# Twelve more of layer 0's weight blocks in split form, with later splits behind fp32 blocks and POOL's clears cut into pieces

## The chip, the cores and the metric

The kernel runs on one core of one Trainium2 chip. The metric is the device time of one launch in microseconds. The core has TensorE (PE, matrix products), VectorE (DVE), ScalarE (ACT), GpSimd (POOL) and SyncE (SP, which here only issues DMAs). Each engine works through its own instruction queue in order; they meet through semaphores.

## The reference

One inference step of a two-layer decoder trunk on 264 token columns (256 of a prompt, 8 samples). Per layer:

```
proj = x @ w_in                                   # 1024 -> 2816, cut into HGRN2 | retention | S5 inputs
o_hg, s_hg = chunked gated linear recurrence      # 6 heads, state 64 x 64
o_rt, s_rt = retention (rotary q, k)              # 6 heads
y5, s5     = complex diagonal S5 scan, gelu, glu
mixed = concat(o_hg, o_rt, y5) @ w_out
x = layer_norm(ALPHA * x + mixed)
ff = square(relu(x @ w_up)) @ w_down
x = layer_norm(ALPHA * x + ff)
```

The outputs are x of both layers' end and the new states. All is fp32, with D_MODEL 1024 and D_FF 4096.

## The kernel before

**Weight blocks.** All dense weights come as 192 blocks of 128 x 1024 fp32 (512 KB), 96 for each layer: steps 0 to 23 are `w_in` (N_IN = 24), then 8 of `w_out`, and the MLP. SP loads block n into `w_raw` slot n % 3 (L480). One step of the schedule is one block; between blocks PE works small "units" of the mixers (levels of the recurrence, scores, transposes, state products), placed by hand in PLAN.

**Two forms.** An fp32 block multiplies `w_raw` with X directly, in 8 matmuls that the profile shows as 16 passes (L971). A split block is written as w = w_high + w_low in fp32r: ACT copies the high part (`split_high`, L1048), DVE subtracts the low part (`split_low`, L1494), and PE does 24 fp32r matmuls (L995 to L997: high by high, high by low of the activations, low by high). Activations are split likewise into `a_high` and `a_low` (L1499). UNSPLIT lists the fp32 blocks of each layer: before, blocks 0 to 21 and 23 of layer 0; layer 1 has none, so all its blocks are split.

**When a block's buffer comes free.** SP loads block n when block n - 3 has been read: a split one as soon as `split_low` is through (`low_ready`), an fp32 one only when PE has finished it (`chunk_done`), see `wait_raw_read`. ACT and DVE issue the split of block n at the head of step n - 2 (AHEAD = 2), in front of that step's own work. That own work, `mixer_work(l, c)` on either engine, evacuates tile c - 1 (gates, Q products, K, V), copies unit results out of the four mix banks and frees these banks for PE (`unit_free`), and frees the three stream banks (`tile_free`).

**DVE's queue in layer 0.** Ahead of step 0: softmax terms, the first table pieces, the eight `a_low` subtractions, more softmax terms. Steps 0 to 9: the S5 tables in pieces (PIECES), and from step 6 on the Q products (L1651), which free the stream banks of tiles 5, 6 and 7. Steps 13 and 14: the two S5 halves (`s5_half`). Steps 10 to 17: the recurrence's levels (L1731 to L1747), rotary, S5 states, gelu argument; steps 16 to 18: `hgrn_sample_add` (L1776), each of which frees a mix bank that `ret_score` (L837) takes later.

**ACT in steps 20 to 22.** Step 20 copies the outputs of `hg_o`, which frees the bank of `hg_state` (L767); step 22 has `head_root` (a square root, with a table load) and eight small copies of the retention's sample outputs (L1245, L1246), for which `ret_mu` (L878) waits. `split_high(22)` and `split_high(24)` stand ahead of these.

**POOL's queue.** Constants and states are loaded by DMAs from POOL; it also clears `s5_near`, `near_packed`, `near` (1536 columns, L520), `st_p` (320, L521) and `level_space` (3072, L522) at the start, each counted in `cleared`. Later it makes the own-value blocks (`affine_select`, L506).

Of the kernel before, what the change touches and what calls it, by code (L numbers as in the profile page):

```python
# [14 lines left out]
DEPTH = 2  # L15
# [5 lines left out]
KT = D_MODEL // 128  # L21
# [24 lines left out]
N_CHUNKS = DOWN_B + 2 * KT  # L46
FF_HALF = FF_TILES // 2
CHUNK = 8 * 128
RAW_SLOTS = 3
SPLIT_SLOTS = 3  # L50
AHEAD = 2
# [113 lines left out]
    if _at[1][0] not in BY_ROW_TILE:  # L165
        UNITS_DONE[_at] = len(UNITS_DONE) + 1
MIX_BANKS = 4
UNSPLIT = ((0, 1, 2, 3, 4, 5, 6, 7, 8, 9, 10, 11, 12, 13, 14, 15, 16, 17, 18, 19, 20, 21, 23), ())
SPLIT = [_n % N_CHUNKS not in UNSPLIT[_n // N_CHUNKS] for _n in range(DEPTH * N_CHUNKS)]
FIRST_SPLIT = [min(_c for _c in range(N_CHUNKS) if _c not in UNSPLIT[_l]) for _l in range(DEPTH)]  # L170
BY_POOL = 3
# [5 lines left out]
def build(nc, xT, weights, vectors, matrices, constants, level_masks, state_hg, state_rt, state_s5,  # L177
          y_out, hg_p_out, rt_p_out, s5_p_out, hg_s_out, rt_s_out, s5_s_out):
    with ExitStack() as ctx:
# [263 lines left out]
        def need(eng, s, n):  # L443

            if n > 0:
                eng.wait_ge(s, n)

        def split_count(n):

            return sum(SPLIT[:n + 1])  # L450
# [37 lines left out]
        def _(pool):  # L488
# [28 lines left out]
            pool.dma_start(consts[:, 0:a], constants[:, 0:a]).then_inc(const_loaded, 16)  # L517
            pool.dma_start(masks[:, :, :], level_masks).then_inc(const_loaded, 16)
            pool.dma_start(s5x0[:, :, :, :, :], state_s5).then_inc(const_loaded, 16)
            pool.memset(near[:, :, :, :, :], 0.0).then_inc(cleared, 1)  # L520
            pool.memset(st_p[:, :, :], 0.0).then_inc(cleared, 1)  # L521
            pool.memset(level_space, 0.0).then_inc(cleared, 1)  # L522
            for l in range(DEPTH):
                if l == 0:
                    pool.wait_ge(chunk_done, 1)
# [502 lines left out]
        def _(act):  # L1028
# [12 lines left out]
            def split_high(n):  # L1041

                if n >= DEPTH * N_CHUNKS or not SPLIT[n]:
                    return
                wait_raw(act, n)
                if n >= SPLIT_SLOTS:
                    act.wait_ge(chunk_done, n - SPLIT_SLOTS + 1)
                act.activation(w_high[:, n % SPLIT_SLOTS, :], w_raw[:, n % RAW_SLOTS, :], ACT.Copy).then_inc(high_ready, 1)  # L1048
# [356 lines left out]
            split_high(1)  # L1405
            for l in range(DEPTH):
                for c in range(N_CHUNKS):
                    split_high(l * N_CHUNKS + c + AHEAD)
                    if c < N_IN:
                        mixer_work(l, c)  # L1410
                        if l and c in (1, 2, 3, 4):
                            ln2_output(l - 1, 2 * c - 2)
                            ln2_output(l - 1, 2 * c - 1)
                        if l == 0 and c == ROT_AT:
                            s5_rot(0)
                        if c == N_IN - 1:
                            mixer_end(l)
                    elif c <= UP_A:
                        ln1_step(l, c)
                    elif c <= DOWN_A:  # L1420
                        m = c - 1 - UP_A
                        linear_sums(l, m)
                        if m == 0:
                            ln1_deviation(l)
                        else:
                            linear_hidden(l, m - 1)
                        if c == DOWN_A:
                            linear_hidden(l, m)
                        if c == UP_A + 3 and l + 1 < DEPTH:
                            act.wait_ge(table_ready, l + 1)  # L1430
                            s5_dt(l + 1)
                        if c == UP_A + 12 and l + 1 < DEPTH:
                            s5_sin(l + 1)
                    elif c < UP_B:
                        if c == DOWN_A + 1:
                            ln1_output(l, 0)
                        elif (c - DOWN_A) % 2 == 0:
                            ln1_output(l, (c - DOWN_A) // 2)
                        if c == DOWN_A + 11 and l + 1 < DEPTH:
                            s5_rot(l + 1)  # L1440
                    elif UP_B < c <= DOWN_B:
                        hidden(l, c - 1 - UP_B + FF_HALF)
                    if c > DOWN_B:
                        ln2_step(l, c)
                    if c in (TABLES_AT + 1, TABLES_AT + 2) and l + 1 < DEPTH:
                        table_copies(l, l + 1, c - TABLES_AT - 1)
                norm(l)
# [3 lines left out]
        def _(dve):  # L1451
# [44 lines left out]
            def split_a(l, part, k, src, m):  # L1496

                dve.wait_ge(ahigh_ready, 24 * l + 8 * part + k + 1)
                put(tt(a_low[:, m, :], src[:, m, :], a_high[:, m, :].bitcast(F32), ALU.subtract), a_ready)  # L1499
# [571 lines left out]

            pieces(2)
            split_low(0)
            for m in range(KT):
                split_a(0, 0, m, X, m)
            split_low(1)
            dve.wait_ge(softmax_exp, 1)
            chain(tt(low[:, 4, :], low[:, 0, :], low[:, 1, :], ALU.add))
# [9 lines left out]

            for l in range(DEPTH):
                for c in range(N_CHUNKS):  # L2090
                    split_low(l * N_CHUNKS + c + AHEAD)
                    if l == 0 and c < TABLE_STEPS:
                        pieces(PIECES[c])
                    if l == 0 and c == TABLE_STEPS:
                        run(first_table)
                        dve.wait_ge(const_loaded, 48)
                    if c < N_IN:
                        mixer_work(l, c)
                        if c == N_IN - 1:
                            mixer_end(l)  # L2100
                    elif c <= UP_A:
                        ln1_step(l, c)
                        if c == UP_A:
                            table = s5_tables(l + 1) if l + 1 < DEPTH else iter(())
                    elif c <= DOWN_A:
                        m = c - 1 - UP_A
                        linear(l, m)
                        if m:
                            hidden_low(l, m - 1)
                        if c == DOWN_A:  # L2110
                            hidden_low(l, m)
                            ln1_scale(l, 0)
                    elif c < UP_B:
                        m = (c - DOWN_A) // 2
                        if (c - DOWN_A) % 2:
                            if m + 1 < KT:
                                ln1_scale(l, m + 1)
                            split_a(l, 2, m, X1, m)
                        else:
                            half_down(l, m - 1)  # L2120
                    elif c <= DOWN_B:
                        if c == UP_B:
                            half_down(l, KT - 1)
                        else:
                            hidden(l, c - 1 - UP_B + FF_HALF)
                            hidden_low(l, c - 1 - UP_B + FF_HALF)
                    else:
                        ln2_step(l, c)
                    if c in TABLE_PIECES:
                        next(table, None)  # L2130
                    if c == TABLES_AT:
                        run(table)
                    if c == N_CHUNKS - 1:
                        residual_down(l, KT - 1)
                norm(l)
# [142 lines left out]
```

## Time and profile before

| | |
|---|---|
| median of 3 runs | 819.85 us (819.52 to 824.4) |
| profiled execution | 821.55 us |
| its span, first to last instruction | 819.5 us |
| mean granted TensorE clock | 0.958 |
| PE busy, share of the span | 754.9 us, 92% |
| DVE busy | 557.6 us, 68% |
| ACT busy | 394.8 us, 48% |
| POOL busy | 43.9 us, 5% |

A busy share is a mean over stages with different limits, so the timelines of the engines in one stretch say more than it does. A row of a timeline gives the start in us, the time taken, the engine, the line of the kernel, the operation, what it writes and reads, and how often it follows itself; in brackets stands how long the engine was idle before and what ended it. A clock of 1.00 is 2.4 GHz, 0.50 is 1.2 GHz.

### The profile page before, as it was taken

The page shows a single profiled execution, that of the slowest core. Times are in us where ns is not written, and L with a number is a line of the kernel's source. Part 1 is how long each engine was busy: PE and PEld are TensorE (multiplying, and loading weights), DVE is VectorE, ACT ScalarE, POOL GpSimd, SP SyncE. Part 2 cuts the span into 40 slices and gives each one's busy share as a digit, 9 for nine tenths or more (in the row PEclk, how much of TensorE's full clock was granted, in tenths as well). Part 3 has the DMA queues.
Part 4 walks back from the last instruction along what each step waited for, and adds up shares of the span by engine and source line. Part 5 has one row for each costly group of instructions (what it writes and reads, how often), then busy time and mean ns, then how long its engine had stood idle before and what let it go on. Part 6 is the DMA issues. An engine that isn't in the chain of part 4 may idle for free. (4 is left out here: it accounts for less than half of the span.)

```text
span 819.5 us, 18059 instructions
## 1 busy us (share of the span) xinstructions
PE 754.9 (92%) x7478; PEld 704.5 (86%) x7478; DVE 557.6 (68%) x1041; ACT 394.8 (48%) x743; POOL 43.9 (5%) x54
## 2 busy tenths in 40 slices
PE   6999798889999999989978899798999999999994
PEld 5788577779999999889978887687899999999994
DVE  7976962246688898884545999635477886666554
ACT  3522214245487654446437525254356874455342
POOL 4000102100000000000021002010000000000001
PEclk9999799888999999999998999899799999999998
DMA  8531112624355555444443232323244555555531
GB/s 343 190 109 54 54 54 93 226 78 141 117 172 164 168 169 178 156 155 154 155 129 104 80 117 94 120 78 112 72 135 154 182 171 190 181 178 169 194 104 53
DMA packets 31009, 113.58 MB, mean 139 GB/s; under 512 B 3568, under 2 KB 3776, under 8 KB 30544
## 3 DMA queue, kind: packets, MB, share of 16 engines
q1 hardware_dynamic: 28368, 101.83, 38.4%
q0 software_dynamic: 1984, 9.52, 3.0%
q8 instruction: 59, 0.97, 0.5%
q10 hardware_dynamic: 576, 1.08, 0.4%
q14 instruction: 22, 0.18, 0.1%
HBM read 108.24 MB, written 4.18 MB: 137 GB/s over the span
## 5 line engine op out<-in xcount | busy, mean ns | idle before, releaser
L1494 DVE TENSOR_TENSOR w_low<-w_raw,w_high 128x1024 fp32r<-128x1024 f32 x169 | 208.5, 1233 | 145.5 <-ACT w_high L1048 144.0
L1048 ACT ACTIVATE w_high<-w_raw 128x1024 fp32r<-128x1024 f32 x169 | 178.1, 1054 | 174.3 <-PE stream L997 146.9
L995 PE MATMUL stream<-a_high,w_high 128*128 128x264 f32 x584 | 176.9, 303 | 14.6 <-DVE a_low L2058 6.3
L996 PE MATMUL stream<-a_low,w_high 128*128 128x264 f32 x584 | 170.9, 293 | 0.0
L997 PE MATMUL stream<-a_high,w_low 128*128 128x264 f32 x584 | 170.3, 292 | 0.0
L995 PE MATMUL stream<-h_high,w_high 128*128 128x264 f32 x512 | 147.8, 289 | 1.3 <-issue 0.6
L996 PE MATMUL stream<-h_low,w_high 128*128 128x264 f32 x512 | 145.2, 284 | 0.0
L997 PE MATMUL stream<-h_high,w_low 128*128 128x264 f32 x512 | 145.0, 283 | 0.0
L995 PEld LDWEIGHTS stream<-a_high,w_high 128*128 128x128 f32 x584 | 115.3, 197 | 21.1 <-issue 16.8
L996 PEld LDWEIGHTS stream<-a_low,w_high 128*128 128x128 f32 x584 | 115.6, 198 | 0.3
L997 PEld LDWEIGHTS stream<-a_high,w_low 128*128 128x128 f32 x584 | 114.8, 197 | 0.0
L971 PE MATMUL stream<-X,w_raw 128*128 128x264 f32 x368 | 91.6, 407 | 8.6 <-DMA w_raw<-in_weights 7.6
L995 PEld LDWEIGHTS stream<-h_high,w_high 128*128 128x128 f32 x512 | 96.4, 188 | 3.2 <-issue 1.4
L996 PEld LDWEIGHTS stream<-h_low,w_high 128*128 128x128 f32 x512 | 96.5, 188 | 0.3
L997 PEld LDWEIGHTS stream<-h_high,w_low 128*128 128x128 f32 x512 | 96.0, 188 | 0.0
L971 PEld LDWEIGHTS stream<-X,w_raw 128*128 128x128 f32 x368 | 72.3, 200 | 23.6 <-DMA w_raw<-in_weights 8.1
L995 PE MATMUL stream<-pre_a,w_high 128*128 128x266 f32 x256 | 74.6, 291 | 1.7 <-DVEq L1473 1.7
L997 PE MATMUL stream<-pre_a,w_low 128*128 128x266 f32 x256 | 73.4, 287 | 0.0
L996 PE MATMUL stream<-pre_x,w_high 128*128 128x266 f32 x192 | 54.9, 286 | 0.0
L995 PEld LDWEIGHTS stream<-pre_a,w_high 128*128 128x128 f32 x256 | 48.4, 189 | 2.3 <-DVEq L1473 2.1
L997 PEld LDWEIGHTS stream<-pre_a,w_low 128*128 128x128 f32 x256 | 48.4, 189 | 0.0
L2029 DVE TENSOR_TENSOR h_low<-h_full,h_high 128x264 fp32r<-128x264 f32 x64 | 27.5, 430 | 18.1 <-ACT h_high L1390 15.7
(373 smaller groups left out, 1020.5 us busy)
## 6 DMA issues: line engine op xcount, KB each, us to landing
w_raw<-in_weights SPq DMA_DIRECT2D x192, 512.0 KB, 3.5
mats<-in_matrices POOLq DMA_DIRECT2D x2, 1024.0 KB, 5.7
S_hg<-in_state_hg POOLq DMA_DIRECT2D x2, 768.0 KB, 7.6
out_hg_s<-S_hg POOLq DMA_DIRECT2D x2, 768.0 KB, 3.7
consts<-in_constants POOLq DMA_DIRECT2D x1, 1484.5 KB, 9.4
X<-in_xT ACTq DMA_DIRECT2D x4, 264.0 KB, 5.1
out_y<-X SPq DMA_DIRECT2D x4, 264.0 KB, 2.1
S_rt<-in_state_rt POOLq DMA_DIRECT2D x2, 512.0 KB, 9.9
```

The costliest lines, as they stand in the source:

```text
L971: mm = pe.matmul(bnk[:, 0:T], w_raw[:, n % RAW_SLOTS, 128 * k:128 * k + 128], X[:, k, :], start=(k == 0), stop=(k == 7))
L995: pe.matmul(bnk[:, 0:width], wh, xh, start=(first and kk == 0), stop=False)
L996: pe.matmul(bnk[:, 0:width], wh, xl, start=False, stop=False)
L997: mm = pe.matmul(bnk[:, 0:width], wl, xh, start=False, stop=(last and kk == 7))
L1048: act.activation(w_high[:, n % SPLIT_SLOTS, :], w_raw[:, n % RAW_SLOTS, :], ACT.Copy).then_inc(high_ready, 1)
L1494: put(tt(w_low[:, n % SPLIT_SLOTS, :], w_raw[:, n % RAW_SLOTS, :], w_high[:, n % SPLIT_SLOTS, :].bitcast(F32), ALU.subtract), low_ready)
L2029: put(tt(h_low[:, m % FF_HALF, :], h_full[:, m % 2, :], h_high[:, m % FF_HALF, :].bitcast(F32), ALU.subtract), h_ready)
```

## The change

UNSPLIT for layer 0 becomes blocks 0 to 4, 6, 7, 9, 10, 12 and 13; blocks 5, 8, 11, 14 to 21 and 23 are split in addition to 22. FIRST_SPLIT of layer 0 goes from 22 to 5 with it. A split whose raw buffer is freed by an fp32 block (n - 3 unsplit: `split_late`) is issued at the head of step n - 1 in place of n - 2, on ACT and DVE alike; this holds for blocks 5, 15 and 16. The eight `a_low` subtractions move from the front of DVE's queue to step 2 of layer 0. POOL clears `near` in four pieces of 384 columns and `level_space` in twelve of 256; `cleared` counts as before.

```diff
-UNSPLIT = ((0, 1, 2, 3, 4, 5, 6, 7, 8, 9, 10, 11, 12, 13, 14, 15, 16, 17, 18, 19, 20, 21, 23), ())
+UNSPLIT = ((0, 1, 2, 3, 4, 6, 7, 9, 10, 12, 13), ())
@@
+        def split_late(n):
+
+            return RAW_SLOTS <= n < DEPTH * N_CHUNKS and not SPLIT[n - RAW_SLOTS]
+
@@ POOL
-            pool.memset(near[:, :, :, :, :], 0.0).then_inc(cleared, 1)
+            for h in range(2):
+                for t in range(2):
+                    m = pool.memset(near[:, h, :, t, :], 0.0)
+            m.then_inc(cleared, 1)
             pool.memset(st_p[:, :, :], 0.0).then_inc(cleared, 1)
-            pool.memset(level_space, 0.0).then_inc(cleared, 1)
+            for at in range(0, 3072, 256):
+                m = pool.memset(level_space[:, at:at + 256], 0.0)
+            m.then_inc(cleared, 1)
@@ ACT
-                    split_high(l * N_CHUNKS + c + AHEAD)
+                    n = l * N_CHUNKS + c
+                    if split_late(n + 1):
+                        split_high(n + 1)
+                    if not split_late(n + AHEAD):
+                        split_high(n + AHEAD)
@@ DVE
             pieces(2)
             split_low(0)
-            for m in range(KT):
-                split_a(0, 0, m, X, m)
             split_low(1)
@@
-                    split_low(l * N_CHUNKS + c + AHEAD)
+                    n = l * N_CHUNKS + c
+                    if split_late(n + 1):
+                        split_low(n + 1)
+                    if not split_late(n + AHEAD):
+                        split_low(n + AHEAD)
+                    if l == 0 and c == max(FIRST_SPLIT[0] - 3, 0):
+                        for m in range(KT):
+                            split_a(0, 0, m, X, m)
```

## Rows read from the trace of the kernel before

**Rows 1.** Busy time by stretch; columns: stretch, length, PE, PEld, DVE, ACT, POOL, clock, DMA
```profile
17.00:40.00 23.00, 22.00 (x98) 18.50 (x99) 21.13 (x63) 11.65 (x24) 0.00 (x0) 1.00 0.61 217
...
155.00:175.00 20.00, 15.28 (x86) 12.47 (x87) 8.19 (x16) 9.44 (x24) 0.00 (x0) 0.79 0.23 92
```

**Rows 2.** Timeline of PE and DVE, layer 0, blocks 2 to 8
```profile
16.95 21.63 PE L971 MATMUL stream<-X,w_raw 128*128 128x264 f32 x96 [1.59 <-DMA w_raw<-in_weights]
39.58 3.83 PE L971 MATMUL stream<-X,w_raw 128*128 128x264 f32 x16 [1.00 <-DVEq L1473]
...
32.67 0.69 DVE L1600 TENSOR_TENSOR scratch<-late,par 128x512 f32<-128x512 f32 x1
...
39.04 0.43 DVE L1651 TENSOR_TENSOR Qg<-Qg,stream 128x264 f32<-128x264 f32 x1
```

**Rows 3.** Waits up to 160 us (total, times, longest); PE's timeline, layer 0, late steps
```profile
ACT w_high L1048 <- DMA w_raw<-in_weights: 20.1, 2, 12.0
...
137.97 0.92 PE L767 MATMUL mix<-V_tok,scratch 128*64 128x64 f32 x24 [2.02 <-ACTq L1039]
...
163.74 3.01 PE L878 MATMUL mix<-MIX,consts 128*128 128x264 f32 x6 [3.35 <-ACT MIX L1246]
```

**Rows 4.** PE's timeline: fp32 block 13 of layer 0, split block 13 of layer 1
```profile
72.47 3.83 PE L971 MATMUL stream<-X,w_raw 128*128 128x264 f32 x16
76.13 1.89 PE L622 MATMUL mix<-scratch,late 128*128 128x64 f32 x16
...
500.03 0.39 PE L995 MATMUL stream<-a_high,w_high 128*128 128x264 f32 x1
...
503.13 0.46 PE L744 MATMUL mix<-scratch 64*32 64x32 f32 x32
```

**Rows 5.** The page's costliest groups: busy us, mean ns of one, idle before
```profile
L1494 DVE TENSOR_TENSOR w_low<-w_raw,w_high 128x1024 fp32r<-128x1024 f32 x169 | 208.5, 1233 | 145.5 <-ACT w_high L1048 144.0
L1048 ACT ACTIVATE w_high<-w_raw 128x1024 fp32r<-128x1024 f32 x169 | 178.1, 1054 | 174.3 <-PE stream L997 146.9
```

**Rows 6.** Timeline of DVE and POOL at the clears (`st_p`'s stands between the two)
```profile
8.94 4.76 DVE L1527 TENSOR_SCALAR par<-par 128x8 f32<-128x8 f32 x1
...
9.37 1.40 POOL L520 MEMSET near<- 128x1536 f32 x1
...
10.99 2.68 POOL L522 MEMSET scratch<- 128x3072 f32 x1
```

**Rows 7.** Timeline of DVE and POOL at the affine_selects
```profile
100.02 1.59 DVE L1756 TENSOR_TENSOR X<-X,consts 128x528 f32<-128x528 f32 x1
...
101.01 3.06 POOL L506 TENSOR_SCALAR_AFFINE_SELECT late<-late 8x1024 f32<-8x1024 f32 x2
```

**Rows 8.** Timeline of DVE and PE, layer 0, steps 12 to 17
```profile
64.74 0.64 DVE L1747 COPY_PREDICATED near_packed<-masks,mix 128x192 f32<-128x192 uint8 x2 [7.89 <-PE mix L744]
...
109.60 0.69 DVE L1776 TENSOR_TENSOR S_hg<-S_hg,mix 128x512 f32<-128x512 f32 x1 [0.93 <-PE mix L777]
...
110.49 0.70 PE L837 MATMUL mix<-QR,KR 32*128 32x256 f32 x4 [0.41 <-DVEq L1473]
```

**Rows 9.** PE's timelines, scores of step 18 in both layers, layer 1's steps 17 and 20
```profile
126.58 0.70 PE L837 MATMUL mix<-QR,KR 32*128 32x256 f32 x4 [0.63 <-ACTq L1039]
...
526.40 0.57 PE L995 MATMUL stream<-a_high,w_high 128*128 128x264 f32 x1
...
530.58 0.70 PE L837 MATMUL mix<-QR,KR 32*128 32x256 f32 x4
...
542.66 0.70 PE L837 MATMUL mix<-QR,KR 32*128 32x256 f32 x4 [1.28 <-ACTq L1039]
...
555.73 0.44 PE L862 MATMUL mix<-scratch,V_tok 128*64 128x128 f32 x4 [1.18 <-DVEq L1473]
```

**Rows 10.** PE's timeline, layer 0, behind block 17
```profile
115.10 1.07 PE L777 MATMUL mix<-late 8*64 8x512 f32 x4
...
117.11 0.70 PE L837 MATMUL mix<-QR,KR 32*128 32x256 f32 x4
```

## Prediction

> **What bounds the kernel.** I read the page's busy shares first: TensorE (PE) leads, VectorE (DVE) and ScalarE (ACT) are far behind. That is a mean over stages. The table by stretches shows what the mean hides: from 17 to 40 us DVE is busy for 21.13 of 23.00 us, nearly as full as PE, and from 155 to 175 us PE is busy for only 15.28 of 20.00 us at a mean clock of 0.79 [rows 1]. So I read the two ends of layer 0's mixer stage in the timelines, asking at each PE wait which engine ends it.
>
> Early, PE runs blocks 2 to 7 without a gap, 21.63 us from 16.95, or 3.6 us each, and block 8 then waits 1.00 us for DVE: its stream bank still holds tile 5, which DVE frees behind the product at 39.04 [rows 2]. Late, PE waits 2.02 us ahead of `hg_state` and 3.35 us ahead of `ret_mu`, both for copies that ACT makes behind a split whose raw block has not landed: those two split waits are 20.1 us of idle ACT, one of them 12.0 us [rows 3]. These two waits are what the change can remove outright.
>
> **What a split block costs and gives.** PE's own price, from start to start of what follows: fp32 block 13, 76.13 - 72.47 = 3.66 us; split block of layer 1, 503.13 - 500.03 = 3.10 us [rows 4]. A converted block saves PE 0.56 us at full clock, twelve blocks 6.7 us. Its price elsewhere is 1.05 us of ACT and 1.23 us of DVE [rows 5], about 1.15 us of DVE when a neighbour's start overlaps its tail. ACT's 12 x 1.05 = 12.7 us fit into its idle time (it is busy for 11.65 of 23 and for 9.44 of 20 us in the two stretches [rows 1]); DVE's need not.
>
> **Part 1: block 5, the moved a_low, and the clears.** Block 5 is now the first split block, so PE needs `a_low` and `w_low` of block 5 from DVE. The eight `a_low` subtractions move from before the softmax to step 2 of the same queue: no work more, none less. `split_low(5)` stands at the head of DVE's step 4, which begins at 32.67 [rows 2]. PE reaches block 5 at 16.95 + 3 x 3.6 = 27.8 us. Left as it is, DVE would deliver at 32.7 + 1.2 = 33.9 us: a wait of 6.1 us. All of DVE's queue stands behind that split (the table pieces, the Q products, level 0), and PE behind these.
>
> What decides is the third edit. One tensor_scalar of only 8 columns starts at 8.94 and ends at 13.70, 0.03 us after POOL's last clear (10.99 + 2.68 = 13.67) [rows 6]. POOL's clears hold it. In pieces, a clear of 256 columns is an estimate of 2.68/3072 x 256 = 0.22 us plus about 0.1, so 0.33 us; near's four pieces of 384 columns 0.44 us. How long DVE waits is not shown and has two ends. Lower: it gets in at the end of the first piece, about 9.8, and its next three such operations wait up to 0.33 us each; gain 13.70 - 9.8 - 0.3 = 3.6 us. Upper: it gets in at no end of a piece; the clears grow by 16 small overheads, about 0.5 us, and DVE is 0.5 us later. For the lower end: the release follows the end of a clear by 0.03 us, and where DVE's tensor_tensor meets POOL's affine_select it starts at 100.02, waits until the next select starts at 101.01 and is done 1.59 us after its start, at 101.61, so it gets in at the end of a select although another is queued [rows 7]. For the upper end: the clears of `near` and `st_p` also ended inside those 4.76 us, and DVE got in at neither. I take the lower end, narrowly, because there are now 16 ends in place of two, and keep the other as the main rival.
>
> The Trainium skill bears on this choice (SBUF — State Buffer, "Who interferes with whom"): the port pair that VectorE shares with GpSimd is locked for a whole instruction, by whichever came first, and a tensor_scalar may use both ports. By that rule DVE gets in at the end of a piece and the sum is the one below; the trace shows the block [rows 6] but not the hand-over at the two ends inside it, and by the trace alone the sum would be the rival's.
>
> With the gain DVE reaches step 4 at 32.67 - 3.6 = 29.1 and delivers at 30.3: PE waits 2.5 us, is then 2.5 - 0.56 = +1.9 us late. DVE's tile-5 product comes at 39.04 - 3.6 + 2 x 1.2 (splits 5 and 8) = 37.9, PE reaches block 8 at 38.58 + 1.9 = 40.5, so the wait of 1.00 goes. Blocks 8 and 11 save 0.56 each: 1.9 - 1.0 - 0.56 - 0.56 = -0.2 us after block 11. ACT's split 5 waits for raw block 5 (freed when block 2 ends, at 20.6) to land, which delays tile 3's sigmoids by a microsecond or so; block 6 needs their bank only at 33. In SP's queue raw 8 now waits for `low_ready` (30.3) and raw 9 stands behind it, which waits for block 6 anyway; in POOL's queue the state loads come 0.5 us later, for step 12.
>
> **Part 2: blocks 14 to 19, where DVE has no room.** Split 14 lies in the 7.89 us in which DVE idles ahead of 64.74. From the first S5 half on, which PE releases, DVE works all but without rest up to `hgrn_sample_add` at 109.60, before which it is idle 0.93 us [rows 8]. The changed queue puts splits 15, 16, 17, 18 and 19 ahead of it: 5 x 1.15 = 5.8 us. Its bank is what `ret_score` 0 and 1 wait for, already 0.41 us today [rows 8]. So PE at 110.49 is late by -0.2 + 5.8 - 0.9 = +4.7 us, and what blocks 14, 15 and 16 save on PE is lost in this wait. The stall of about 6 us drops PE's clock: in layer 1, behind such a wait, a split block begins at 526.40 and ends at 530.58, 4.2 us instead of 3.10 [rows 9]: +1.1. Block 17: -0.56. Total +5.2 at its end.
>
> The next pair of scores starts 117.11 - 115.10 = 2.0 us after block 17 ends [rows 10]. Now the chain behind that end is split_high(20) 1.06, split_low(20) 1.23, `hgrn_sample_add(2)` 0.69 and some 0.2 of hops, 3.2 us: +1.2, total +6.4. Block 18: +5.9.
>
> **Part 3: blocks 19 to 23, where waits go.** Step 18's ACT wait grows as in layer 1, where all blocks are split (1.28 against 0.63 us here) [rows 9]: +0.6; step 20's `ret_o` waits 1.18 us for DVE there and does not here: +1.2. Blocks 19, 20, 21 and 23: -2.2. Raw blocks 22 and 24 are now freed by `low_ready`, two steps before, so ACT has no raw wait: -2.02 and -3.35 [rows 3]. `ret_mu` took 3.01 us for six fp32 passes at half clock behind that stall [rows 3]; at the 0.23 us a pass of block 13 (3.66/16) it takes 1.6: -1.4. The spread units behind it begin at half clock too: -0.4, an estimate. Sum: 5.9 + 0.6 + 1.2 - 2.2 - 5.4 - 1.4 - 0.4 = -1.7 us.
>
> The late-split rule itself adds no work: it only applies behind fp32 blocks (5, 15, 16) and keeps ACT's step from waiting. Layer 1's queues are unchanged, so the rest is shifted by the same -1.7. The profiled execution took 821.55 us for a span of 819.5; the median of the runs shown is 819.85, 1.7 lower. Against its own time the sum gives 819.8; on the median, 818.
>
> **The rivals.**
> *No hand-over* (0.37). DVE gets in at no end of a clear. `split_low(5)` then ends at 32.7 + 0.5 + 1.2 = 34.4, PE waits 6.6 us, starts cold (+1.1), and is +7.1 after block 5, against +1.9; the 1.00 wait goes here too. The end is 5.2 us later: +3.5, so 823.4. This is the case on the other side: it decides from a DVE gain below 1.9 us (half of the 3.6) on, where the sum passes zero.
> *The raw wait is not what holds ret_mu* (0.10). ACT's step 22 also has a table load and eight small copies; if these come as late as before, the 3.35 and the 1.4 stay: -1.7 + 4.8 = +3.1, 823.0. Against it: ACT was idle 12.0 us ahead of them [rows 3].
> *DVE's lateness hurts less and the clock holds* (0.14). If PE keeps its clock at block 17 (-1.1), if block 22, in the 0.79 stretch [rows 1], is spared the same 1.1, and if the 4.7 us are halved (-2.4), the change gives -1.7 - 4.6 = -6.3, 813.5. For it: a shorter wait ahead of the scores also keeps the clock.
> The forecast has 0.39.
>
> **Range and chances.** The cases span 813.5 to 823.4; unsized clock drops of 1.1 us each (two or three more) and a measurement spread of 1 to 2 us widen it: 811 to 826. The forecast with its own bounds is 815 to 821. About 1% (8 us) is what a measurement of this kernel can tell from no change. Faster by more needs the third rival and two microseconds more: 0.12. Slower by more needs no hand-over together with colder blocks behind each new wait: 0.10. Within 1%: 0.78.
>
> **What would show it.** After: L1527's long tensor_scalar is gone (hand-over) or still ends with the last clear (none). PE's wait ahead of the first L995 is 2.5 us, or 6.6. A new DVE wait of 4 to 6 us stands ahead of `ret_score` 0 and 1 (L837). No ACT wait on raw blocks after step 15; `ret_mu` follows block 22 without a gap and takes 1.6 us. Blocks 5 to 23 in split form take 3.1 us. The prediction fails if DVE between the S5 halves and the sample adds shows idle time that could take the splits, or if PE's waits there are ended by ACT.

## Result and profile after

Ten runs of the changed kernel have a median of 830.17 us (826.8 to 831.19), ten of the kernel before, taken beside them, 822.4 us (819.52 to 829.92). The ratio is 1.0087, 95% interval 1.0061 to 1.0114: slower, 12 us above the forecast of 818.0 and outside its range of 811 to 826. Of these 12 us, 2.6 belong to the kernel before: the forecast started from its median of three runs, 819.85, and ten runs give 822.4. By the ratio the change costs 7.2 us where 1.85 of gain was forecast, 9 us off. The profiled execution has a span of 829.5 us, 10.0 more than before, at a mean clock of 0.946. It is the slowest of its ten runs, and the profiled one of before (821.55) lies under the median of ten, so the two traces show some 3 us more of a loss than the ratio.

Lines have moved: the fp32 block is L980, the split one L1004 to L1006, `split_low` L1507, `split_high` L1057, `a_low` L1512, the 8-column tensor_scalar L1540, the clears L526 to L530, `hgrn_sample_add` L1789, `ret_score` L846 and L849, `ret_mu` L887, the spread units L903.

First the clears, DVE's and POOL's timelines after:

```profile
9.00 5.18 DVE L1540 TENSOR_SCALAR par<-par 128x8 f32<-128x8 f32 x1
...
9.29 1.51 POOL L526 MEMSET near<- 128x384 f32 x4
10.72 0.38 POOL L528 MEMSET st_p<- 128x320 f32 x1
11.03 3.12 POOL L530 MEMSET scratch<- 128x256 f32 x12
```

The tensor_scalar ends at 9.00 + 5.18 = 14.18, 0.03 us behind the last of the clears (14.15). It got in at none of the 16 ends before that. Its row begins at 9.00, ahead of the first clear's at 9.29 (8.94 and 9.37 in [rows 6]); what holds it in those 0.3 to 0.4 us the rows don't show. Against [rows 6] it takes 0.42 us longer: the pieces brought only their overheads.

What follows from it, timelines of DVE and PE after, steps 4 to 6:

```profile
33.15 1.23 DVE L1507 TENSOR_TENSOR w_low<-w_raw,w_high 128x1024 fp32r<-128x1024 f32 x1
...
34.47 0.56 PE L1004 MATMUL stream<-a_high,w_high 128*128 128x264 f32 x1 [6.71 <-issue]
34.83 0.42 PE L1005 MATMUL stream<-a_low,w_high 128*128 128x264 f32 x1
```

PE waits 6.71 us for block 5's low part, then works at half clock (granted clock 0.50 from 34.5 to 40): a pass of 0.42 us where it is 0.28 at full clock, and the block takes 5.62 us (34.47 to 40.09). The table by stretches, for three of them (columns as in [rows 1]):

```profile
17.00:40.00 23.00, 16.29 (x73) 14.41 (x73) 20.25 (x54) 10.54 (x20) 0.00 (x0) 0.79 0.51 190
...
120.00:140.00 20.00, 16.28 (x82) 14.39 (x83) 10.49 (x19) 2.33 (x5) 0.00 (x0) 0.60 0.16 53
155.00:175.00 20.00, 19.02 (x179) 16.73 (x178) 6.30 (x10) 7.73 (x22) 3.20 (x6) 0.91 0.56 207
```

From 17 to 40 us PE is busy for 16.29 us where it was 22.00 [rows 1]. From 120 to 140 us its clock is 0.60; before it is 1.00 there. From 155 to 175 us it is better off than before: 19.02 busy at 0.91, against 15.28 at 0.79. The last two stretches don't hold the same blocks in both kernels, since PE is later by 10 us and more; the table of blocks below compares like with like.

The middle, timelines of DVE and PE after:

```profile
99.93 2.35 DVE L1507 TENSOR_TENSOR w_low<-w_raw,w_high 128x1024 fp32r<-128x1024 f32 x2
...
113.15 1.22 DVE L1507 TENSOR_TENSOR w_low<-w_raw,w_high 128x1024 fp32r<-128x1024 f32 x1
...
119.95 1.23 DVE L1507 TENSOR_TENSOR w_low<-w_raw,w_high 128x1024 fp32r<-128x1024 f32 x1
121.28 0.69 DVE L1789 TENSOR_TENSOR S_hg<-S_hg,mix 128x512 f32<-128x512 f32 x1
...
94.67 1.21 PE L753 MATMUL mix<-scratch 64*32 64x32 f32 x96 [5.34 <-DVEq L1486]
...
115.86 1.07 PE L786 MATMUL mix<-late 8*64 8x512 f32 x4 [1.67 <-DVEq L1486]
118.25 0.63 PE L676 MATMUL mix<-consts,KR 128*128 128x128 f32 x4 [1.32 <-DVEq L1486]
...
122.17 1.22 PE L846 MATMUL mix<-QR,KR 32*128 32x256 f32 x4 [3.29 <-DVEq L1486]
123.75 0.59 PE L1004 MATMUL stream<-a_high,w_high 128*128 128x264 f32 x1
...
132.82 1.22 PE L846 MATMUL mix<-QR,KR 32*128 32x256 f32 x4 [1.54 <-DVEq L1486]
```

The sample add for which the first scores wait stood at 109.60 [rows 8] and stands at 121.28, right behind split 19. The scores' wait of 0.41 us has become 3.29, and the scores themselves take 1.22 us, where 0.70 is full clock. The rest of the lateness stands in waits for DVE ahead of that one: 5.34 us at 94.67 (3.24 before), 1.67 at 115.86 and 1.32 at 118.25. Blocks 17 and 18 behind them run from 123.75 to 129.40 and from 134.40 to 139.88, 5.65 and 5.48 us, where the same form takes 3.17 in blocks 14 and 19. Blocks 15 and 16 go the other way: in fp32 form they took 5.63 and 5.48 us before, now 3.90 and 3.17, which is 2.9 us more than the 0.56 each that the form saves. Like the form's own saving, it is lost in the wait for the add.

The late steps, timelines of ACT, DVE and PE after:

```profile
174.23 1.06 ACT L1057 ACTIVATE w_high<-w_raw 128x1024 fp32r<-128x1024 f32 x1 [3.41 <-PE stream L1006]
175.30 1.28 ACT L1108 ACT_TABLE_LOAD   x1
176.60 0.39 ACT L1108 ACTIVATE late<-stream 128x264 f32<-128x264 f32 x1
...
177.02 0.49 DVE L1777 SCALAR_TENSOR_TENSOR late<-late,vecs,stream 128x264 f32<-128x264 f32 x1 [0.48 <-ACT late L1108]
177.66 1.58 DVE L1902 TENSOR_TENSOR MIX<-MIX,mix 128x264 f32<-128x264 f32 x3
...
173.97 1.50 PE L887 MATMUL mix<-MIX,consts 128*128 128x264 f32 x6
175.39 0.87 PE L903 MATMUL mix<-consts,head_sd 128*64 128x128 f32 x12
...
178.29 1.67 PE L903 MATMUL mix<-consts,head_sd 128*64 128x128 f32 x24 [2.03 <-DVEq L1486]
```

`ret_mu` follows block 22 without a wait and takes 1.50 us; before it waited 3.35 us and took 3.01 [rows 3]. The 2.02 us ahead of `hg_state` are gone too. New is a wait of 2.03 us one unit later. Its chain begins at the end of block 22: split 25 on ACT, a table load of 1.28 us, the copy of `late`, DVE's sum and then the subtractions that free the bank.

PE's lateness against before, at the start of each block, tells where the 10 us of the traces are (from the two timelines of PE):

| block | 9 | 12 | 14 | 15 | 16 | 17 | 18 | 19 | 20 | 21 | 22 | 23 | `w_out` 0 |
|---|---|---|---|---|---|---|---|---|---|---|---|---|---|
| us | +7.0 | +6.4 | +6.4 | +8.8 | +8.0 | +12.4 | +16.4 | +18.3 | +15.4 | +16.0 | +14.6 | +10.2 | +9.6 |

The early part loses 6.4 us, the middle 11.9, the late part wins 8.7.

### The profile page after: what moved, and what is told of

It reads as the page before. It is cut to its first block and busy times, and to the rows that moved or that the text cites. A ratio compares the mean times of both kernels' runs of the same rounds, so it can differ in the third digit from the quotient of the medians.

```text
span 829.5 us, 18305 instructions
## 1 busy us (share of the span) xinstructions
PE 751.5 (91%) x7574; PEld 710.1 (86%) x7574; DVE 572.0 (69%) x1053; ACT 406.9 (49%) x755; POOL 44.1 (5%) x68
## 5 line engine op out<-in xcount | busy, mean ns | idle before, releaser
L1507 DVE TENSOR_TENSOR w_low<-w_raw,w_high 128x1024 fp32r<-128x1024 f32 x181 | 223.0, 1233 | 157.0 <-ACT w_high L1057 155.2
L1057 ACT ACTIVATE w_high<-w_raw 128x1024 fp32r<-128x1024 f32 x181 | 190.9, 1054 | 225.6 <-PE stream L1006 206.8
L1004 PE MATMUL stream<-a_high,w_high 128*128 128x264 f32 x680 | 209.7, 308 | 20.6 <-issue 6.7
L1005 PE MATMUL stream<-a_low,w_high 128*128 128x264 f32 x680 | 202.1, 297 | 0.0
L1006 PE MATMUL stream<-a_high,w_low 128*128 128x264 f32 x680 | 201.3, 296 | 0.0
L1004 PEld LDWEIGHTS stream<-a_high,w_high 128*128 128x128 f32 x680 | 137.4, 202 | 28.7 <-issue 24.0
L1004 PE MATMUL stream<-h_high,w_high 128*128 128x264 f32 x512 | 147.8, 289 | 1.4 <-issue 0.5
L1006 PE MATMUL stream<-h_high,w_low 128*128 128x264 f32 x512 | 145.0, 283 | 0.0
L1005 PEld LDWEIGHTS stream<-a_low,w_high 128*128 128x128 f32 x680 | 137.8, 203 | 0.3
L1006 PEld LDWEIGHTS stream<-a_high,w_low 128*128 128x128 f32 x680 | 137.0, 202 | 0.0
L1004 PEld LDWEIGHTS stream<-h_high,w_high 128*128 128x128 f32 x512 | 96.4, 188 | 3.4 <-issue 1.6
L1006 PEld LDWEIGHTS stream<-h_high,w_low 128*128 128x128 f32 x512 | 96.0, 188 | 0.0
L1004 PE MATMUL stream<-pre_a,w_high 128*128 128x266 f32 x256 | 74.6, 291 | 1.7 <-DVEq L1486 1.7
L1006 PE MATMUL stream<-pre_a,w_low 128*128 128x266 f32 x256 | 73.4, 287 | 0.0
L1004 PEld LDWEIGHTS stream<-pre_a,w_high 128*128 128x128 f32 x256 | 48.4, 189 | 2.3 <-DVEq L1486 2.1
L980 PE MATMUL stream<-X,w_raw 128*128 128x264 f32 x176 | 43.1, 404 | 7.5 <-DMA w_raw<-in_weights 7.5
L1006 PEld LDWEIGHTS stream<-pre_a,w_low 128*128 128x128 f32 x256 | 48.4, 189 | 0.0
L980 PEld LDWEIGHTS stream<-X,w_raw 128*128 128x128 f32 x176 | 34.6, 200 | 13.9 <-DMA w_raw<-in_weights 7.9
```

The lines of the kernel that those rows point to most:

```text
L980: mm = pe.matmul(bnk[:, 0:T], w_raw[:, n % RAW_SLOTS, 128 * k:128 * k + 128], X[:, k, :], start=(k == 0), stop=(k == 7))
L1004: pe.matmul(bnk[:, 0:width], wh, xh, start=(first and kk == 0), stop=False)
L1005: pe.matmul(bnk[:, 0:width], wh, xl, start=False, stop=False)
L1006: mm = pe.matmul(bnk[:, 0:width], wl, xh, start=False, stop=(last and kk == 7))
L1507: put(tt(w_low[:, n % SPLIT_SLOTS, :], w_raw[:, n % RAW_SLOTS, :], w_high[:, n % SPLIT_SLOTS, :].bitcast(F32), ALU.subtract), low_ready)
```

## Experiments

Ratios are to the kernel before, run beside each; "after" is the changed kernel.

**ScalarE writes the zeros.** `near` and `level_space` are cleared by ACT behind its first copies, in place of POOL.

```diff
@@ POOL (st_p's memset, between the two loops, stays)
-            for h in range(2):
-                for t in range(2):
-                    m = pool.memset(near[:, h, :, t, :], 0.0)
-            m.then_inc(cleared, 1)
-            for at in range(0, 3072, 256):
-                m = pool.memset(level_space[:, at:at + 256], 0.0)
-            m.then_inc(cleared, 1)
@@ ACT
+            zero_in = X[:, :, :].rearrange("p a b -> p (a b)")[:, 0:1536]
+            act.activation(near[:, :, :, :, :].rearrange("p a b c d -> p (a b c d)"), zero_in, ACT.Copy, scale=0.0).then_inc(cleared, 1)
+            act.activation(level_space[:, 0:1536], zero_in, ACT.Copy, scale=0.0)
+            act.activation(level_space[:, 1536:3072], zero_in, ACT.Copy, scale=0.0).then_inc(cleared, 1)
```

> The changed kernel, but ScalarE writes the zeros of near and level_space (three activations behind the a_high copies) and POOL clears neither. Theory A (POOL's clears hold DVE's tensor_scalar, and through it block 5): the 5.18 us tensor_scalar at 9.0 is gone, DVE reaches split_low(5) some 4.9 us earlier, at about 28.3 in place of 33.15, PE waits about 1.7 us ahead of block 5 in place of 6.71 and does not drop its clock there (block 5 takes 3.1 us, not 5.6). Block 12 then starts at about 66, not 72.5, and the total is 6 to 7 us under the changed kernel, about equal to the kernel before. Rival B (DVE is held by something else, the software DMAs say): the long tensor_scalar stays and the time is that of the changed kernel.

Measured: 822.35 us, ratio 0.9977 (0.9946 to 1.0008). Timelines of DVE, POOL and PE of this kernel:

```profile
9.55 0.40 DVE L1537 TENSOR_SCALAR par<-par 128x8 f32<-128x8 f32 x1
...
9.53 0.38 POOL L524 MEMSET st_p<- 128x320 f32 x1
...
29.83 0.36 PE L997 MATMUL stream<-a_high,w_high 128*128 128x264 f32 x1 [1.29 <-issue]
```

The tensor_scalar takes 0.40 us, held by the one clear that is left. The wait ahead of block 5 is 1.29 in place of 6.71, the block takes 3.14 us in place of 5.62, and block 12 starts at 65.06, 7.4 us earlier. Theory A met, and the total fell by more than its 6 to 7 us. The middle's loss is as large as in after: 11.7 us, from -1.1 at block 12 to +10.6 at block 19 (138.05). So the clears on POOL account for about 8 us of the total (7.8 by the medians, 9.0 by the ratios), and the middle's loss doesn't come from them.

**Gaps between the pieces.** POOL waits for three more of DVE's steps ahead of each piece of `level_space`; the work is the same.

```diff
-            for at in range(0, 3072, 256):
+            for i, at in enumerate(range(0, 3072, 256)):
+                pool.wait_ge(dve_step, 29 + 3 * i)
```

> The changed kernel, but each of the 12 clears of level_space waits until DVE has done three more steps of its early chain, so POOL is idle between pieces. Theory A (POOL's shared access is handed over only when POOL's queue really runs dry, not at the border of two clears that follow each other): the tensor_scalar that took 5.18 us ends with the clear of st_p, at about 11.1 (2.1 us), and later ones wait at most 0.35 us each; PE's wait ahead of block 5 falls from 6.7 to about 4 us, total 3 to 5 us under the changed kernel. Rival B (a clear in the queue holds DVE whatever the gap): tensor_scalar still ends only with the last clear, which then can't start, so the kernel would be at least as slow as the changed one. Rival C (hand-over at each border, but the clears were never the cause): as the changed kernel.

Measured: 825.53 us, ratio 1.0011 (0.9975 to 1.0048). Timelines of DVE, POOL and PE:

```profile
9.65 1.78 DVE L1541 TENSOR_SCALAR par<-par 128x8 f32<-128x8 f32 x1
...
9.58 1.51 POOL L526 MEMSET near<- 128x384 f32 x4
11.02 0.38 POOL L528 MEMSET st_p<- 128x320 f32 x1
11.49 0.31 POOL L531 MEMSET scratch<- 128x256 f32 x1
12.09 0.31 POOL L531 MEMSET scratch<- 128x256 f32 x1 [0.29 <-DVE low L2092]
...
31.49 0.56 PE L1005 MATMUL stream<-a_high,w_high 128*128 128x264 f32 x1 [3.02 <-issue]
```

The tensor_scalar stays out through the four back-to-back pieces of `near` and the clear of `st_p`, and ends at 11.43, 0.03 us behind that clear (11.40), where POOL's queue first stands still (0.09 us, up to 11.49). Behind it the small ones take 0.17 to 0.19 us each; the longest is one of 1024 columns, 0.88 us beside a clear, where the next takes 0.69. So DVE got in where POOL paused and not where clears followed each other, as theory A said. PE waits 3.02 us, a microsecond less than its 4, and block 5 takes 4.44.

**Whole clears.** After, with `level_space` and, likewise, `near` cleared in one instruction each.

```diff
-            for at in range(0, 3072, 256):
-                m = pool.memset(level_space[:, at:at + 256], 0.0)
-            m.then_inc(cleared, 1)
+            pool.memset(level_space, 0.0).then_inc(cleared, 1)
```

> The kernel after with its clears made whole again, in one instruction each. Theory A (no border between pieces lets VectorE in; the pieces only add small overheads): the 8-column tensor_scalar ends about 0.5 us earlier than the 14.18 of the kernel after, still just behind the last clear; the wait ahead of block 5 is 6.2 to 6.7 us; ratio to before within 0.002 of the kernel after's 1.0087. Theory B (the pieces let VectorE in somewhere later, so that they gave part of what they promised): the wait ahead of block 5 is over 7.5 us and the ratio is above 1.011.

Measured: 830.13 us, ratio 1.0077 (1.0049 to 1.0104). DVE's and POOL's timelines:

```profile
8.54 4.92 DVE L1535 TENSOR_SCALAR par<-par 128x8 f32<-128x8 f32 x1
...
10.75 2.68 POOL L526 MEMSET scratch<- 128x3072 f32 x1
```

It ends at 13.46, with the last clear again (13.43). The ratio is theory A's. The wait ahead of block 5 was 6.88 us, 0.2 above what it said, since PE had reached block 5 at 27.40 and not at 27.77. Cutting the clears changed nothing in the total that can be measured.

**Splits 19 to 23 only.** The early and the middle blocks are fp32 again; `a_low` then stands in step 16. Blocks 19 to 21 come behind fp32 blocks here and are split a step later than in after; this also holds for the runs below that leave 16 to 18 in fp32 form.

```diff
-UNSPLIT = ((0, 1, 2, 3, 4, 6, 7, 9, 10, 12, 13), ())
+UNSPLIT = ((0, 1, 2, 3, 4, 5, 6, 7, 8, 9, 10, 11, 12, 13, 14, 15, 16, 17, 18), ())
```

> The changed kernel with UNSPLIT 0 to 18 in layer 0: only blocks 19 to 23 are split, a_low moves to step 16. Theory A (the late part gains, the early part and the stretch of blocks 14 to 18 lose): no raw waits of ACT in steps 20 to 23, no 2.0 us wait ahead of hg_state, no 3.35 us wait ahead of ret_mu, four blocks 0.5 us shorter: 6 to 9 us under the kernel before, ratio 0.990 to 0.993. Rival B (the late part gains nothing either, since DVE or the clock takes it back): ratio 0.998 to 1.002.

Measured: 818.41 us, ratio 0.9923 (0.989 to 0.9956). Theory A met. One row of DVE's timeline shows what holds it back:

```profile
102.39 3.72 DVE L1512 TENSOR_TENSOR a_low<-X,a_high 128x264 fp32r<-128x264 f32 x8
```

The eight subtractions now lie in DVE's full stretch; PE waits 1.13 and 2.07 us behind them, block 17 takes 6.10 us, and block 19 starts at 132.67, +5.2.

**The same, with `a_low` in step 12**, in DVE's idle time ahead of the first S5 half [rows 8].

```diff
-                    if l == 0 and c == max(FIRST_SPLIT[0] - 3, 0):
+                    if l == 0 and c == 12:
```

> As the run with blocks 19 to 23 split, but the eight a_low subtractions stand in step 12, where DVE idled 7.9 us before, and not in step 16. Theory A (DVE has no room from step 13 to hgrn_sample_add(1) in step 17; there a_low cost 3.7 us, put that add 2.2 us later and cost a clock drop at block 17): the add stands near 109.6 minus a little, PE waits about 0.4 us ahead of the first scores, block 17 takes 3.8 us and not 6.1, and the kernel is 3 to 5 us faster than with a_low in step 16: ratio to the kernel before 0.985 to 0.989. Rival B (a_low's place is hidden anyway and the drop at block 17 came by itself): ratio 0.991 to 0.994 as there.

Measured: 814.49 us, ratio 0.9898 (0.9862 to 0.9934), block 19 at 126.73, 0.7 us earlier than before. The gain of 8.4 us is the late part, but for those 0.7 us, which come from moving `a_low`: block 12 starts 1.6 us earlier than before. Theory A was right on the total's direction (3.9 us under the run above) and wrong on the way: the add stands at 107.21, 2.4 us earlier than before, but the scores wait 1.82 us and not 0.4, and block 17 takes 5.51 us and not 3.8. So `a_low` in step 16 didn't cause the clock drop at block 17 by itself.

**Splits 17 to 23**, `a_low` in step 12: the run above and two more splits.

```diff
-UNSPLIT = ((0, ... 14, 15, 16, 17, 18), ())
+UNSPLIT = ((0, ... 14, 15, 16), ())
```

> Blocks 17 to 23 split, a_low in step 12. Theory A (each split that stands ahead of hgrn_sample_add(1) costs DVE's full stretch 1.15 us, past the 0.9 us of idle time, and a wait of PE over about 3 us costs a clock drop of 2.5 us besides): two splits, so the first scores wait 1.5 to 2 us in place of 0.4, without a clock drop, blocks 17 and 18 save 1.1 us, and the wait ahead of the second scores grows by about 1.3 us: 1 to 3 us over the run with 19 to 23 split and a_low in step 12. Rival B (blocks 17 and 18 gain as 19 to 23 do): 1 us or more under it.

Measured: 817.92 us, ratio 0.9942 (0.9909 to 0.9974), 3.4 us over the run above. PE's timeline:

```profile
107.97 0.63 PE L676 MATMUL mix<-consts,KR 128*128 128x128 f32 x4 [1.32 <-DVEq L1486]
...
111.89 1.23 PE L846 MATMUL mix<-QR,KR 32*128 32x256 f32 x4 [3.29 <-DVEq L1486]
```

The same 3.29 us stand ahead of the scores as in after, though nothing early is late here and only two splits are in front (split 19, behind fp32 block 16, comes after the add); block 17 behind it takes 4.81 us. Block 19 starts at 131.53, 4.8 us later than in the run above. Theory A has the direction, against rival B, but its wait of 1.5 to 2 us without a clock drop was too mild.

**Splits 14 to 23**, `a_low` in step 11 (the diff is against the run with splits 19 to 23).

```diff
-UNSPLIT = ((0, ... 14, 15, 16, 17, 18), ())
+UNSPLIT = ((0, ... 12, 13), ())
```

> The changed kernel with UNSPLIT 0 to 13 in layer 0: blocks 14 to 23 split, 5, 8 and 11 not, a_low at step 11. Theory A (the loss is the sum of an early part of 6 to 7 us and a part of about 12 us in steps 14 to 18, less about 8 us won in steps 19 to 23): PE is not late at block 12, is late by 10 to 13 us at block 19, and the total is 3 to 5 us over the kernel before (ratio 1.004 to 1.006), 5 to 7 us under the changed one. Rival B (only the early part loses, the later lateness was its echo): 5 to 8 us under the kernel before.

Measured: 820.08 us, ratio 0.9963 (0.993 to 0.9997). It met neither theory. Block 19 starts at 137.87, +10.4, as theory A said, with blocks 17 and 18 at 5.65 and 5.55 us as in after. The late part wins 9.1 us behind it, much as in after (8.7): `w_out` 0 starts at 175.90, 1.35 us later than before. Yet the span is 818.3 us, 1.2 shorter than before. The 2.6 us between lie behind `w_out` 0, where the edits don't reach: from there to the end the traces of this document take 640.4 to 646.6 us, and no edit orders them. That spread of single executions is why the total missed theory A while its blocks met it, and why the starts of blocks say more here than one total.

**After without splits 15 to 18.** Blocks 5, 8, 11, 14 and 19 to 23 stay split.

```diff
-UNSPLIT = ((0, 1, 2, 3, 4, 6, 7, 9, 10, 12, 13), ())
+UNSPLIT = ((0, 1, 2, 3, 4, 6, 7, 9, 10, 12, 13, 15, 16, 17, 18), ())
```

> The kernel after with blocks 15 to 18 in fp32 form again; 5, 8, 11, 14 and 19 to 23 stay split, a_low in step 2, the clears in pieces. Theory A (the splits 15 to 18 in VectorE's full stretch are what makes blocks 14 to 19 lose 12 us): block 19 starts at about 133 to 135 (145.69 in the kernel after), and the ratio is about 0.995 to 0.999, 8 to 11 us under the kernel after. Theory B (once the early part is late by 6.7 us, the middle stays late by itself, through the queues' order): block 19 is later than 140 and the ratio above 1.002.

Measured: 819.82 us, ratio 0.9956 (0.9933 to 0.9979). Timelines of DVE and PE:

```profile
118.67 0.69 DVE L1789 TENSOR_TENSOR S_hg<-S_hg,mix 128x512 f32<-128x512 f32 x1 [4.94 <-PE mix L786]
...
119.56 0.70 PE L846 MATMUL mix<-QR,KR 32*128 32x256 f32 x4 [0.42 <-DVEq L1486]
...
120.42 3.83 PE L980 MATMUL stream<-X,w_raw 128*128 128x264 f32 x16
```

DVE is idle for 4.94 us ahead of the add for which the scores wait: PE is what it waits for. The wait ahead of the scores is 0.42 us again, block 17 runs at full clock, and block 19 starts at 136.51, +9.1 in place of +18.3. The middle still loses 3.1 us behind the late early part; splits 15 to 18 bring the other 9. Those 3.1 us aren't the clock of blocks 15 and 16 (5.25 and 5.93 us, 5.63 and 5.48 before); two waits between small units, at 96.47 and 108.62, are 0.9 and 1.0 us longer than before, and the rest wasn't followed. Theory A met; the block's start was 1.5 us past its window.

**After without the late-split rule** (`split_late` always false).

```diff
-            return RAW_SLOTS <= n < DEPTH * N_CHUNKS and not SPLIT[n - RAW_SLOTS]
+            return False
```

> The changed kernel without the later splits behind fp32 blocks: splits 5, 15 and 16 are issued two steps ahead, as all others. Theory A (the later split pays where ACT and DVE would stand waiting for a raw block, and costs where DVE is behind and PE waits for it): at block 5 DVE issues the split 2.1 us earlier and PE waits about 4.5 in place of 6.7 us; at step 13 DVE waits for raw block 15 ahead of the first S5 half, 3 to 4 us. Net 0 to 2 us slower than the changed kernel. Rival B (the late rule does nothing, within 1 us); rival C (it is what made the changed kernel slow: 3 us or more faster without it).

Measured: 830.52 us, ratio 1.0099 (1.0067 to 1.0131): no difference from after that can be told. The traces differ all the same. `split_low(5)` is early and PE waits 4.17 us in place of 6.71; but split 15, issued a step sooner, waits for a raw buffer that fp32 block 12 frees late (DVE's timeline):

```profile
77.40 1.23 DVE L1507 TENSOR_TENSOR w_low<-w_raw,w_high 128x1024 fp32r<-128x1024 f32 x1 [5.17 <-ACT w_high L1057]
```

The 5.17 us hold back the first S5 half, and PE meets a new wait of 4.69 us at 85.10. In the traces the rule has cost 4.0 us by block 12 (72.49 against 68.51), 2.5 of it in that wait, and saves 4.9 from there to block 14 (85.29 against 86.24). Theory A met in its parts, with 5.17 us where it had 3 to 4.

**A better version.** ACT's clears, splits 8, 11 and 19 to 23, which puts `a_low` in step 5 (the clears' lines as in the first experiment):

```diff
-UNSPLIT = ((0, 1, 2, 3, 4, 6, 7, 9, 10, 12, 13), ())
+UNSPLIT = ((0, 1, 2, 3, 4, 5, 6, 7, 9, 10, 12, 13, 14, 15, 16, 17, 18), ())
```

> ScalarE clears near and level_space; blocks 8, 11 and 19 to 23 split; a_low in step 5. Theory A (with the clears off POOL, DVE has 4.8 us to spare early, which pays for a_low and two splits): no DVE wait ahead of block 8, two blocks 0.5 us shorter, so 1 to 3 us under the run with 19 to 23 split and a_low in step 12: ratio 0.982 to 0.987. Rival B (ScalarE's three clears of 4.7 us, or the earlier state loads that now share the DMA engines with the first weight blocks, take it back): ratio as there or above it.

Measured: 811.99 us, ratio 0.9875 (0.9811 to 0.994). With block 14 added (the same diff without the 14):

> ScalarE's clears, splits 8, 11, 14 and 19 to 23: one more, block 14, than in the run that splits 8, 11 and 19 to 23 (0.9875). Theory A (split 14 lies in VectorE's idle 7.9 us ahead of the first S5 half and costs nothing there): 0 to 1 us under that run, ratio 0.986 to 0.988. Theory B (every split ahead of the full stretch arrives in it as lateness): 1 to 2 us over it, ratio 0.989 to 0.990.

Measured: 811.11 us, ratio 0.9868 (0.9824 to 0.9913). And with block 5 added as well:

> As the run with splits 8, 11, 14 and 19 to 23, and block 5 split as well, with a_low in step 2. With ScalarE's clears the wait ahead of block 5 was 1.29 us. Theory A (block 5 saves 0.5 on TensorE and costs 1.3 of wait and the splits and a_low ahead of the tables, 2 to 3 us at block 12): 1 to 3 us over that run. Theory B (what it costs early is idle time of TensorE later anyway): within 0.5 us of it.

Measured: 813.01 us, ratio 0.9884 (0.9837 to 0.9931). The three intervals lie over each other and over that of splits 19 to 23 with `a_low` in step 12 (0.9862 to 0.9934). The medians stand as theory A put them in both cases (0.9 us under, then 1.9 us over), but the runs tell none of these four apart, so that ScalarE's clears and splits 8, 11 and 14 add to the late part's gain isn't shown. All four beat both kernels.

## Why the prediction was wrong

Setting the ratios in a row prices the parts: the late part alone gives 0.9898 (-8.4 us). The early part with POOL's clears and split 14 brings it to 0.9956 (+4.8). Splits 15 to 18 bring it to 1.0087 (+10.8). The forecast had -8.2, -0.2 and about +6.7. Each step between two ratios is uncertain by some 3 us, and the traces, by the start of `w_out` 0 (-7.8, +1.6, +9.6), share the same loss out as 9.4 and 8.0.

| step of the prediction | forecast | measured |
|---|---|---|
| PE's wait ahead of block 5 | 2.5 us (rival 6.6) | 6.71 |
| block 5 behind it | 3.1 (rival 4.2) | 5.62 |
| wait of block 8 (1.00) | gone | gone |
| after block 11 | -0.2 (rival +5.0) | +6.4 |
| added from there to the scores | +4.9 | +5.3 (11.7 - 6.4) |
| wait ahead of the scores | about 6 us | 3.29, behind 1.67 and 1.32 |
| blocks 17 and 18 | one of them +1.1 | +2.5 and +2.4 |
| at block 19 | +6.5 | +18.3 |
| `hg_state`'s and `ret_mu`'s waits | gone | gone |
| `ret_mu` | 1.6 | 1.50 |
| spread units behind it | -0.4 | new wait of 2.03 |
| late part in all (from block 19 on) | -8.2 | -8.7 |

**The step that failed** is the choice of the lower end for DVE's wait on the clears: the gain of 3.6 us, and with it the wait of only 2.5 us ahead of block 5. The tensor_scalar ended with the last clear, DVE gained nothing, and PE waited 6.71 us. The rival "No hand-over" is what happened, and its 6.6 us of wait was within 0.1. [rows 6] already had the answer as far as it went: DVE got in at neither of the two ends inside the long wait. The argument against it came from [rows 7], where DVE's tensor_tensor is let in between two affine_selects. That is another pair of operations, and it doesn't carry over. How the two pairs differ inside wasn't tested. By the Trainium skill (SBUF — State Buffer, "Who interferes with whom") the shared ports are locked for the whole instruction of whoever came first, from which the text concluded that a shorter instruction is a shorter wait. The traces don't bear out this conclusion: DVE got in at 0 of 16 ends in after, at 0 of 2 with whole clears, at none of the four ends between the first five clears of the run with gaps, and then at POOL's first pause. Nor do the rows say that POOL came first: in before and after the tensor_scalar's row begins ahead of the first clear's.

**The term that was mis-sized** is the clock. The prediction took 1.1 us, once, for a split block behind a stall of about 6 us, from layer 1's block of 4.2 us [rows 9]. That block stands behind a wait of 3.17 us, in the row that [rows 9] leaves out (before, PE's timeline):

```profile
525.24 1.51 PE L667 MATMUL mix<-consts,scratch 128*128 128x128 f32 x6 [3.17 <-DVEq L1473]
```

In after three blocks behind new waits, 5, 17 and 18, cost 2.3 to 2.5 us each. For block 5 the runs order them by the wait ahead: behind 1.29 us it takes 3.14, behind 3.02 us 4.44, behind 4.17 us 4.68, behind 6.71 us 5.62. The wait alone doesn't set it: behind the same 3.29 us block 17 took 4.81 us with splits 17 to 23 and 5.65 in after, and behind the same 1.54 us of scores block 18 took 3.16 us in the run with gaps and 5.48 in after. What does set it in these cases is open.

With the no-hand-over rival the prediction's own sum is +3.5 us on the kernel before (it took a cold block 5 at 1.1 us), and the traces have +9.6 at `w_out` 0. The 6.1 us between are mostly clock: 1.4 in block 5, 3.8 in 17 and 18, 0.5 in the scores. This second miss doesn't need the first: with ScalarE's clears PE waits 1.29 us ahead of block 5, less than the forecast's 2.5, and the middle still loses 11.7 us where 6.7 were forecast.

PE's wait at 94.67 also grew, from 3.24 us before to 5.34; it is 3.40 without splits 15 to 18. Split 15, 1.22 us of DVE at 86.62, stands ahead of it; the other 0.7 us aren't explained, and how such waits and the clock share the middle's loss wasn't separated.

**What held.** The queue argument of part 2 was right: five splits of 1.22 us ahead of the sample add, less 0.93 of idle, gives 5.2; DVE reached that add 11.7 us later than before, 6.4 of it being the early part. It holds with nothing late early as well: with splits 14 to 23 PE is 1.0 us early at block 14 and 3.8 late at the scores, 4.8 in all. With two splits ahead of the add (17 to 23) it says 1.5, and 2.4 were measured. Only the place was wrong: a wait of 4 to 6 us was to stand ahead of the scores, and 3.29 did, the rest of the lateness lying in the waits before it. Part 3 was right in place: the raw waits were what held `hg_state` and `ret_mu`, and the rival that doubted it falls. Its size is right in part by luck. The sum left out the chain of block 22's end, split 25 and the table load; it had been hidden under 3.35 + 3.01 us of `ret_mu`. So the stretch from block 22 to 23 won 4.35 us and not 5.15, and the three steps ahead of it 1.1 us more than forecast.

**Still open** is what sets the clock of blocks 17 and 18, and whether the four best versions differ. No run moves the clears to ScalarE and leaves the splits as before.

## What to carry to other kernels

A block form that is cheaper on the bound engine pays only where the engine that prepares it has idle time ahead of its next deadline: here blocks 19 to 23 gave about 8 us, and four blocks in VectorE's full stretch took 8 to 11 back. Price every new wait of TensorE with the slow block behind it, which here cost nothing behind 1.29 us, 1.3 behind 3.02 and 2.5 behind 6.71, but also 2.5 behind 3.29. If a GpSimd instruction holds VectorE up, as the clears did here, give its work to another engine (ScalarE's writes held nothing here) or leave real pauses; cutting it into pieces that followed each other gained nothing.

## What the runs showed of the hardware

- An 8-column tensor_scalar of DVE stayed out through 17 POOL memsets that followed each other (5.18 us) and was done 0.03 us behind the last. With pauses of 0.28 us and more between memsets of 0.31 us such small operations took 0.17 to 0.19 us, and one of 1024 columns 0.88 in place of 0.69. While ACT wrote the same zeros (3 x 1.47 us), small ones took 0.17 to 0.22 us.
- DVE's tensor_tensors of 3 and 8 columns took 0.16 to 0.17 us beside the memsets of the run with gaps, as anywhere.
- Cutting 3072 columns into twelve memsets cost 3.12 us in place of 2.68, 0.04 us for each of the 11 cuts.
- The granted clock was 0.50 (1.2 GHz) in the block behind a wait of 6.71 us, which took 5.62 us, and 1.00 behind a wait of 1.29 us, where the same block took 3.14.
- One execution differs from the next even where the program is the same: from `w_out` 0 of layer 0 to the end, where no edit reaches, the fourteen traces take 640.4 to 646.6 us.
